# One mixer of a two-block transformer, its projections, compression, attention and recurrence placed between one another in a new order

## What is computed

```
def hybrid_mixer(h, w_in, cmp_pos_k, ..., lower_bound, hg_norm, w_out):
    parts = jnp.split(h @ w_in, IN_SPLITS, axis=-1)      # 27 panels of 128 columns
    nq, k_c, v_c, k_s, v_s, k_w, v_w, gl, hq, hf, hi, hg = parts
    o_nsa = nsa_group(nq, k_c, v_c, k_s, v_s, k_w, v_w, gl, ...)
    o_hg = hgrn2_group(hq, hf, hi, hg, lower_bound, hg_norm)
    return jnp.concatenate([o_nsa, o_hg], axis=-1) @ w_out
```

```
def step(state, inp):
    b = jnp.cumsum(lf, axis=2)
    a = jnp.einsum('bhtd,bhtsd,bhsd->bhts', qc, decay, kc)
    o_intra = jnp.einsum('bhts,bhsv->bhtv', a, vc)
    o_inter = jnp.einsum('bhtd,bhdv->bhtv', qc * jnp.exp(b), state)
    new_state = exp(b_last) * state + einsum('bhsd,bhsv->bhdv', kc * exp(b_last - b), vc)
```

## Time and profile before

| | us |
|---|---|
| median of 3 runs | 3269.1 (3268.27 to 3269.39) |
| profiled execution, its time | 3270.03 |
| profiled execution, its span | 3268.0 |
| TensorE busy | 2983.4 (91% of the span), mean clock 0.945 |
| VectorE, ScalarE, GpSimd busy | 1804.2, 1029.6, 844.8 |
| second mixer, its four stages | 2353.16 to 2867.44 |

### The profile page before, as it was taken

One profiled execution on the slowest core, in us unless ns is written; L12 is line 12 of the kernel. 1 busy time (PEld: TensorE's weight loads), 2 busy tenths in 40 slices (PEclk: granted clock), 3 DMA queues, 4 the chain that ended last, 5 costly groups with the idle time before them and its releaser, 6 DMA issues. The chain is left out here.

```text
span 3268.0 us, 41012 instructions
## 1 busy us (share of the span) xinstructions
PE 2983.4 (91%) x14322; PEld 2521.2 (77%) x14322; DVE 1804.2 (55%) x3734; ACT 1029.6 (32%) x1475; POOL 844.8 (26%) x511
## 2 busy tenths in 40 slices
PE   7669779999989999989999998999886998889997
PEld 6438668788868888879999996888765776768885
DVE  5566336756767775038888875443341445554423
ACT  3212313233234444223333333222211333132221
POOL 0013200344523333457666620000022212100000
PEclk9869889999989999989999999999986998899998
DMA  4003222344425555469999972333230212023331
GB/s 142 18 32 116 102 80 83 127 135 135 142 100 183 183 187 189 145 227 375 366 351 355 352 271 91 97 97 97 86 135 26 75 46 94 20 97 97 96 98 63
DMA packets 179308, 466.71 MB, mean 143 GB/s; under 512 B 21729, under 2 KB 71521, under 8 KB 177634
## 3 DMA queue, kind: packets, MB, share of 16 engines
q1 hardware_dynamic: 155490, 372.56, 34.3%
q0 software_dynamic: 22528, 67.19, 5.4%
q10 hardware_dynamic: 1152, 25.17, 1.8%
HBM read 395.44 MB, written 69.21 MB: 142 GB/s over the span
## 5 line engine op out<-in xcount | busy, mean ns | idle before, releaser
L54 PE MATMUL cb_y<-cb_g_hi,cb_b_hi 128*128 128x384 f32 x1024 | 343.2, 335 | 15.0 <-DVE cb_b_lo L1743 15.0
L55 PE MATMUL cb_y<-cb_g_lo,cb_b_hi 128*128 128x384 f32 x1024 | 342.9, 335 | 0.0
L56 PE MATMUL cb_y<-cb_g_hi,cb_b_lo 128*128 128x384 f32 x1024 | 342.8, 335 | 0.0
L186 DVE TENSOR_TENSOR ffn_lo<-ffn_raw,ffn_hi 128x1024 fp32r<-128x1024 f32 x132 | 161.4, 1226 | 273.6 <-ACT ffn_hi L182 273.5
L54 PE MATMUL ffn_bank<-x_hi,ffn_hi 128*128 128x512 f32 x704 | 277.7, 394 | 25.2 <-DVE x_lo L122 23.1
L55 PE MATMUL ffn_bank<-x_lo,ffn_hi 128*128 128x512 f32 x704 | 275.7, 392 | 0.0
L56 PE MATMUL ffn_bank<-x_hi,ffn_lo 128*128 128x512 f32 x704 | 275.4, 391 | 0.0
L491 POOL TENSOR_TENSOR bs_lo<-bs_raw,bs_hi 128x1024 fp32r<-128x1024 f32 x72 | 174.8, 2429 | 320.4 <-ACT bs_hi L468 320.4
L54 PE MATMUL bs_ps<-x_hi,bs_hi 128*128 128x512 f32 x576 | 232.3, 403 | 14.8 <-POOL bs_lo L491 14.8
L182 ACT CAST ffn_hi<-ffn_raw 128x1024 fp32r<-128x1024 f32 x132 | 138.0, 1048 | 301.4 <-PE ffn_bank L56 260.0
L1722 ACT CAST cb_b_hi<-cb_b_raw 128x1024 fp32r<-128x1024 f32 x128 | 134.6, 1052 | 297.8 <-PE cb_y L56 264.6
(11 more groups left out here) (461 smaller groups left out, 6666.7 us busy)
## 6 DMA issues: line engine op xcount, KB each, us to landing
cb_b_raw<-in_peer_v SPq DMA_DIRECT2D x128, 512.0 KB
ffn_raw<-in_gu SPq DMA_DIRECT2D x88, 512.0 KB, 3.6
bs_raw<-in_peer_u SPq DMA_DIRECT2D x72, 512.0 KB, 3.6
rs_raw<-in_peer_u SPq DMA_DIRECT2D x56, 512.0 KB, 3.6
routing<-br_out ACTq DMA_DIRECT2D x8, 3072.0 KB, 9.0
cb_route<-routing SPq DMA_DIRECT2D x32, 768.0 KB
cb_unit<-hidden SPq DMA_DIRECT2D x128, 192.0 KB
ffn_raw<-in_down SPq DMA_DIRECT2D x44, 512.0 KB, 3.6
```

The source lines that it names most:

```text
L54: pe.matmul(out, w_high, x_high, start=first, stop=False)
L55: pe.matmul(out, w_high, x_low, start=False, stop=False)
L56: return pe.matmul(out, w_low, x_high, start=False, stop=last)
L186: dve.tensor_tensor(lo[:, k % R, :], raw[:, k % R, :], hi[:, k % R, :].bitcast(F32), ALU.subtract).then_inc(split, 1)
```

## The change

The second mixer becomes three stages.

1. `project_and_compress`: norm and all 27 panels in one loop with 3 buffers for weights. What stage 2 did is cut into small steps that come behind certain panels on each engine (`TURN_AT`, `PART_AT`, `GELU_AT`, `SCORE_AT` and so on). The compression's first-layer weights are loaded as 8 parts of 1 MB each into memory that later holds the projections. The activations of the recurrent branch and the decay are made here too. The projections stay in SBUF.
2. `attend_and_recur`: the same 64 attention units without the stream, and beside them, at unit numbers written out by hand, the steps of the recurrence (`V_AT`, `SAME_AT`, `LEVEL_AT`, `K_AT`, `WRITE_AT`, `TILE_AT`, `MEAN_AT`, `Y_AT`, `O_AT`), with two PSUM banks instead of six. The multiplication of the keys in `double` goes to GpSimd, and ScalarE copies the result out of PSUM before it is normalised. The bias of a unit is one table of distances for all heads; the slope is in the keys, queries and the exponential's scale.
3. `project_onto` with 8 whole panels.

The core of the diff:

```diff
-                norm_and_project(nc, "p2", hT, x_hi, x_lo, d["mix_norm"], d["w_nsa"], proj, plain, load_w1k, rstd[:])
-                compress_and_attend(nc, proj, ident, w1k, w1_landed, vsel, vwin, gates, bias, o_tok, d)
...
-                stream = PanelStream(c, "p3", d["w_hg"], x_hi, x_lo, d["hg_proj"], None, rstd[:])
...
-        hgrn_stage(nc, d["hg_proj"], o_tok, ident, d["lower_bound"], d["out_norm"], d["w_out"], x_hi, x_lo, hT)
+        project_and_compress(nc, hT, x_hi, x_lo, d, proj, hg, f, qp, rstd, vsel, vwin, gates, o_tok, ident, far)
...
+            attend_and_recur(nc, att, c, hg, f, qp, ident, d["out_norm"], o_tok, x_hi, x_lo)
+
+    project_onto(nc, "wo2", x_hi, x_lo, d["w_out"], hT)
```

TensorE's program in the first new stage:

```diff
+    TURN_AT = {6: (0, 1), 7: (2, 3)}
+    PART_AT = 8
+    GELU_AT = PART_AT + N_PARTS - 1
+    HTURN_AT, KC_AT, SCORE_AT = GELU_AT + 1, GELU_AT + 2, GELU_AT + 3
...
+                for k in range(n):
+                    panel(k)
+                    if k == 1:
+                        norm.tensor(pe)
+                    for t in TURN_AT.get(k, ()):
+                        turn(t)
+                    if 0 <= k - PART_AT < N_PARTS:
+                        hidden_part(k - PART_AT)
+                    if k == HTURN_AT:
+                        turn_hidden()
+                    if k == KC_AT:
+                        keys_and_values()
+                    t = k - SCORE_AT
+                    if 0 <= t < TILES:
+                        score(t)
+                    if 0 <= t - 2 < TILES:
+                        result(t - 2)
+                    if 0 <= t - 1 < TILES:
+                        turn_weights(t - 1)
```

Loads, and ScalarE's and VectorE's order in that stage:

```diff
+                for k in range(R, n):
+                    load(k)
+                    if k < R + 6:
+                        load_part(k - R)
+                    if k in (14, 15):
+                        load_part(k - 8)
...
+                for k in range(5, n):
+                    behind(k - 4)
+                    high_part(k)
...
+                for k in range(EARLY, n):
+                    behind(k - 1)
+                    take(k)
+                    if k + R < n:
+                        low_part(k + R)
```

The places of the recurrence's steps, the part that GpSimd takes over, and TensorE's program beside the units:

```diff
+    V_AT, SAME_AT, LEVEL_AT = 0, 4, 8
+    K_AT = (25, 26, 27)
+    WRITE_AT = (29, 31, 34)
+    TILE_AT = (28, 33, 36, 38)
+    MEAN_AT = 40
+    Y_AT = 44
+    O_AT = (22, 40, 53)
...
+            for m in range(LEVELS):
+                for e in range(2):
+
+                    pool.wait_ge(S["scored"], 2 * m + e + 1)
...
+                    pool.tensor_tensor(early, early, both[:, :, 1:2].broadcast_to(early.shape), ALU.mult
+                                       ).then_inc(S["keys_doubled"], 1)
...
+            def beside(i):
+                if 0 <= i - V_AT < TILES:
+                    turn_values(i - V_AT)
+                if 0 <= i - SAME_AT < 4:
+                    same_token(i - SAME_AT)
+                if level_of(i):
+                    level(*level_of(i))
+                if i in K_AT:
+                    turn_keys(K_AT.index(i))
+                if i in WRITE_AT:
+                    write(WRITE_AT.index(i))
+                if i in TILE_AT:
+                    whole_tile(TILE_AT.index(i))
+                if 0 <= i - Y_AT < TILES:
+                    turn_result(i - Y_AT)
+                if i in O_AT:
+                    turn_attended(O_AT.index(i))
+            att.tensor(pe, beside)
+            turn_attended(TILES - 1)
```

More of the change, by code:

```diff
@@ L508, with __init__ @@
 class Attention:
[L515 to L519, removed]
+    def __init__(self, c, name, units, ident):
+        self.units, self.ident = units, ident
         n = len(units)
@@ L535, in __init__, with vector @@
         self.gated_units = 0
-    def vector(self, dve):
+    def vector(self, dve, beside=None):
         n = len(self.units)
@@ L613, in tensor @@
                 last.then_inc(self.turned, 1)
-            if self.stream is not None and i < n:
-                at = i % self.every * self.share
-                self.stream.tensor(pe, 0, i // self.every, slice(at, at + self.share))
+            if beside is not None:
+                beside(i)
             if i >= 2:
@@ L1919, in compress_and_attend @@
         o_ps = c.ps("cp_ops", [P, SEQ])
-        pT_ps = [c.ps(f"cp_pTps{i}", [P, SEQ]) for i in range(2)]
-        s_ps = [turn_ps, [c.ps(f"cp_s{i}", [P, SEQ]) for i in range(2)]]
+        norm = NormStage(c, "p2", hT, d["mix_norm"], o_ps, o_tok[:, 0:2], None, o_tok[:, 2:4], rstd[:])
         S = {x: c.sem(f"cp_{x}") for x in (
-            "w", "w1v", "hturned", "hidden", "cleared", "const", "biases", "turned", "copied", "gates", "gated", "blocks", "hid", "gelu", "kc", "kcopied",
-            "scored", "seq", "shifted", "exped", "weights", "pturned", "pcopied", "out", "stored")}
@@ L1926, in compress_and_attend @@
-        n_small = 3
+            "high", "split", "product", "taken", "plain_high", "plain_split",
+            "w", "hturned", "hidden", "cleared", "const", "scaling", "biases", "turned", "copied", "gates", "gated", "blocks",
+            "part_used", "hid", "gelu", "kc", "kcopied", "scored", "seq", "shifted", "exped", "weights", "pturned", "pcopied",
+            "out", "stored", "lb", "lb_shift", "lb_exp", "sig", "nsig", "silu", "gated_silu", "f", "key", "query")}
+        landed = [c.sem(f"p_landed{i}") for i in range(R)]
@@ new lines, in _ @@
+                for h in range(NSA_HEADS):
+                    part = slice(h // 4 * NSA_HD, (h // 4 + 1) * NSA_HD)
+                    dve.memset(qscale[part, h % 4:h % 4 + 1], 1.0 / slope_of(h)).then_inc(S["scaling"], 1)
+                dve.wait_ge(norm.gain_landed, 16)
+                low_part(0)
+                for kc in range(KC):
+                    plain_low(kc)
+                    if kc == 3:
+                        low_part(1)
+                low_part(2)
+                dve.wait_ge(S["lb"], 16)
@@ new lines, in unit @@
+        def unit(t, h, branch):
+            part = slice(h // 4 * NSA_HD, (h // 4 + 1) * NSA_HD)
+            w, at = (t + 1) * P, (TILES - 1 - t) * P
+            keys, values = ((KSEL, vsel), (KWIN, vwin))[branch - 1]
+            return dict(q=proj[part, NQ0 + h % 4, t * P:(t + 1) * P], k=proj[part, keys, :w], width=w,
+                        bias=far[:, at:at + w], v=lambda b: values[:, b, part], dv=NSA_HD, add=True,
+                        gate=gates[:, t, 3 * h + branch:3 * h + branch + 1], scale=float(NSA_HD) ** -0.5 * slope_of(h),
+                        out=o_tok[:, t, h * NSA_HD:(h + 1) * NSA_HD])
@@ L2623, in final_norm @@
+        with ExitStack() as attending:
+            c = Chip(nc, attending)
+            att = Attention(c, "att2", [unit(t, h, branch) for t in range(TILES) for branch in (1, 2)
+                                        for h in range(NSA_HEADS)], ident)
+            attend_and_recur(nc, att, c, hg, f, qp, ident, d["out_norm"], o_tok, x_hi, x_lo)
+    project_onto(nc, "wo2", x_hi, x_lo, d["w_out"], hT)
 def final_norm(nc, hT, gain, out):
```

1108 lines of the change are left out of this document (553 added, 555 removed).

## The result

The changed kernel took 3286.05 us (median of five runs, 3279.64 to 3295.97), the kernel before 3268.27 us beside it (3266.51 to 3269.39). The ratio is 1.0058, with a 95% interval of 1.0042 to 1.0073: slower by 17.8 us, where 57 us less had been forecast. The profiled execution took 3287.4 us with a span of 3285.7; TensorE is busy for 3050.3 us (93%), where it was 2983.4 us (91%) for the same dense work.

A forecast was written before the change was run, and what follows sets the result against it. TensorE, busy 91% of the span, was taken as the bound. Stages of 220.9, 181.8 and 54.3 us sum to 457.0 against 514.3, 57.3 less, giving 3212 us; range 3195 to 3240.

The forecast's parts named there:

- rival 1: Attention block: without the dense matmuls it runs at half clock, 3342 us in place of 3212; chance 0.05.
- Against it: the first mixer's attention, with the same chain and no dense work, ran at 1.00.: Argument against half clock in the attention block: TensorE was busy there for 13.66 of 14 us.
- So did the level steps (26.5 of 29.4 us).: Argument against half clock: the old kernel's level steps also ran at clock 1.00, TensorE busy 26.5 of 29.4 us.
- In the wide units TensorE has no waits at all.: Argument against half clock in the attention block's wide units, where TensorE was taken as the bound.
- First stage, 220.9: 27 panels with the compression in their gaps: old first stage 74.9, 16 more panels 89.1, small steps 50.4, rest; 220.9 us.
- rival 3: First stage: the compression isn't hidden and all 30 us of the old stage's idle time return, 3242 us; chance 0.08.
- Output projection, 54.3: Last stage: takes the 54.3 us of the first mixer's, same function, shapes and panel count, with its lead-in bare.
- Attention block at full clock, 181.8: Second stage: 64 attention units 114.2 us, level steps 29, other recurrent steps, norm, crossings and clearing; 181.8 us.
- Rival 2: Attention block: VectorE and GpSimd block each other, or the hand-placed steps cross, 3241 us; chance 0.17.

The follow-up runs named there:

- the run of the units alone: The changed kernel with the recurrent steps (levels, state, norm) left out from between the 64 attention units, part of the result missing: 3237.95 us.

## Why the prediction was wrong, point by point

The step that failed: the sum priced all small matmuls of the attention block at full clock (2.48 us for a 512-wide unit, 3.45 for a level step), and the argument under rival 1, with its chance of 0.05, was the reason for that. The clock in the block was 0.58, a 512-wide unit took 4.65 us and most level steps 4.87 to 5.93, and the time was 3286 in place of 3212.

- **"Against it: the first mixer's attention, with the same chain and no dense work, ran at 1.00."** The row is right for its 14 us (in the 14 us before them, with TensorE busy for 8.40, the clock was 0.76), and "the same" was wrong. The first mixer's scores cover 128 rows and its value products 128 columns (`128*128` and `128x128` in the lines below, from 344 to 358 us of the kernel before); here both are 64. The runs changed exactly these: 128 rows alone took the 512-wide units from 0.50 to 1.00, 128 columns alone took nearly the whole block to 0.94.

```profile
L625 PE MATMUL att_o<-m_vv,att_probsT 128*128 128x128 f32 x40 | 6.0, 281 | 0.0
...
L603 PE MATMUL att_s<-m_kT,m_proj 128*128 128x384 f32 x8 | 3.2, 487 | 0.0
```

- **"So did the level steps (26.5 of 29.4 us)."** This was misread. The stretch wasn't without dense work: 37 dense matmuls of the output projection's half panels stood between the level steps, as its groups show (2776.5 to 2805.9 us of the kernel before). It gave no evidence for level steps without dense matmuls. Between attention units with 64-column value products they stood at 0.50, even with 128-row scores. A stretch's clock was read as belonging to one kind of instruction, when it belonged to the mixture.

```profile
L2306 PE MATMUL hg_s<-hg_qp,hg_kr 128*128 128x64 f32 x160 | 18.6, 274 | 0.6 <-DVE hg_pairs L2501 0.6
L56 PE MATMUL hg_out<-x_hi,hg_lo 128*128 128x512 f32 x13 | 5.1, 393 | 0.0
L54 PE MATMUL hg_out<-x_hi,hg_hi 128*128 128x512 f32 x12 | 5.0, 414 | 0.0
L55 PE MATMUL hg_out<-x_lo,hg_hi 128*128 128x512 f32 x12 | 4.7, 389 | 0.0
```

- **"In the wide units TensorE has no waits at all."** True, and no evidence: it was busy for 20.00 of 20 us at 0.50. I took the compression's 0.50 for the effect of its waits (27.8 of 42.8 us busy); but its matmuls are small in rows or columns too (`31*128 31x64`, `64*128 64x31`), and no run here tells the two apart. The rule of the Trainium skill that I weighed there ("TensorE: Matmul & The Clock Gate", section "HAM oscillation — how this bites in real kernels") named thin matmuls and waits; the clock came out as this rival had it, but with next to no waits (one fall, at 2723, came with a wait of 1.76 us; the 85 us of half clock before 2690 had none). The Trainium skill ("TensorE: Matmul & The Clock Gate", section "Why this matters for your kernels") advises to keep TensorE continuously busy to reach the full clock. The trace disagrees: busy for 20.00 of 20 us in row after row, it stayed at half, so the measurement decides.
- **Rival 1's price, 3342**, was for half clock nearly throughout. Measured: 4.65 us for 4.96 in a 512-wide unit, and 1.00 between 2700 and 2720 us; together 72 us over the forecast block and not 130, or 96 us over the shortest block measured at nearly full clock (157.6). Its threshold ("half clock over somewhat under half of the block") wasn't tested: at a mean clock of 0.58, half clock held for some 84% of the block (estimated from the mean of the two levels).
- **First stage, 220.9**: 223.2. The compression is hidden; rival 3 didn't happen (207.98 us of TensorE in 223.16). **Output projection, 54.3**: 53.98.
- **Attention block at full clock, 181.8**: with the clock restored at least cost it is 157.6, so I was 24 us too high. A 512-wide unit takes 2.19 us for 2.48, though with 128-row scores; a level step 3.08 for 3.45 (40.0/13). The largest part lies in units 22 to 47: 58.3 us, where the forecast has 45.8 for the plain units and 24 for the recurrent steps (up to unit 53), the norm and the crossings, which the chain hid in part; the interval at unit 40 is 3.95 us.
- **Rival 2**: its mechanism exists (0.77 us in place of 0.16), at one small instruction a step, and costs the kernel nothing that was measured. The Trainium skill ("GPSIMD Engine Reference", section "8. Key points") has contention at two SBUF inputs; the trace agrees, and the form with one tensor input escapes it.

Where the gain went, then: the merge of the stages does save what was claimed and more, and TensorE's clock takes it back. With 128-row scores in all units, and 18 spare matmuls and wider value products around the level steps, the same order of work takes 3191.67 us.

## What to carry to other kernels

Before dense work is taken out from between small matmuls, look at the granted clock of a stretch that has exactly the mixture that will be left, shapes included, and list what ran in that stretch before it is called as evidence; a busy TensorE without waits is no sign of full clock. When the rows show TensorE full and the clock at 0.50, try making its operations larger (zero rows, columns that nobody reads, a spare dense matmul a unit). Here it cost less than it gave: 160 value products of doubled width took 80 us off. And where a lone slow row appears, such as a one-column multiplication of 0.77 us, test what it is worth before it is called a bound.

## What the runs showed of the hardware

- TensorE stayed at its 1.2 GHz level for 205 us (the run of the units alone, clock 0.50) while busy for 198.5 of them. Each of three edits to the changed kernel (0.58), of which none takes work from any engine, brought it to 2.4 GHz over most of the block: scores over 128 rows (mean clock 0.80), value products of 128 columns (0.94), one dense matmul a unit (0.95). What the chip counts isn't known from these runs.
- The same program does not always get the same clock: the changed kernel's five runs had means of 0.926 to 0.931 and spread over 16 us, where the kernel before has 3. With the 128-row scores and wide value products the level units of one execution took first 4.5 to 5.0 us each and then 2.9.
- A VectorE multiplication of two 128 x 1 operands in SBUF ended with GpSimd's running one (0.77 us in place of 0.16); one with the second operand as a scalar took 0.21 us beside the same GpSimd operation.
- At 2.4 GHz a 512-wide unit took 2.53 us with scores over 64 rows and 2.19 with scores over 128 (wide value products in both); with 64 rows the next weights were loaded only behind the scores.
